# The first RMS norm of an encoder block, made on token rows in the load stage instead of on channel rows beside the first projection

## What is computed

```python
def rms_norm(x, gain):
    y = xf * lax.rsqrt(jnp.mean(xf * xf, axis=-1, keepdims=True) + NORM_EPS)
    return y * gain

def encoder_layer(h, ...):
    u = rms_norm(h, norm_mix)
    proj = u @ w_in
    dn_qkv, dn_z, dn_b, dn_a, at_q, at_k, at_v, gate_dn, gate_at = split_cols(proj, IN_SPLITS)
    ...
    merged = jax.nn.sigmoid(gate_dn) * y_dn + jax.nn.sigmoid(gate_at) * y_at
    h = h + merged @ w_o
```

## Time and profile before

| | us |
|---|---|
| median of 3 runs (3501.0 to 3505.09) | 3501.05 |
| the profiled execution | 3500.08 |
| its span, first to last instruction | 3498.3 |
| TensorE busy (84%) | 2953.3 |
| VectorE busy (46%) | 1623.2 |
| ScalarE busy (26%) | 899.2 |
| GpSimd busy (9%) | 313.1 |

### The profile page before, as it was taken

How to read it: one execution, slowest core, us unless ns; L and a number is a source line. 1 busy time by engine, 2 the same in 40 slices (tenths; PEclk the granted TensorE clock), 3 DMA queues, 4 the chain that set the end, 5 groups by cost and what they waited for, 6 DMA issues and landing times. The chain is left out here.

```text
span 3498.3 us, 41643 instructions
## 1 busy us (share of the span) xinstructions
PE 2953.3 (84%) x17373; PEld 2476.4 (71%) x17373; DVE 1623.2 (46%) x2172; ACT 899.2 (26%) x1233; POOL 313.1 (9%) x409
## 2 busy tenths in 40 slices
PE   5884216989476994899799989999999999999999
PEld 3663105878365773799788877888888888888877
DVE  5431322895934583243476733433333343434542
ACT  2553001111022451122244445123111111111331
POOL 0000110000000000666200022011000000000110
PEclk7887557999788996899999999999999999999999
DMA  2211455236132222766301046321111111111112
GB/s 89 69 45 43 114 140 163 82 126 180 43 80 68 75 93 79 195 181 183 113 31 46 16 158 235 126 80 36 37 37 37 37 37 42 38 37 37 46 52 58
DMA packets 298337, 295.58 MB, mean 84 GB/s; under 512 B 52635, under 2 KB 254006, under 8 KB 297270
## 3 DMA queue, kind: packets, MB, share of 16 engines
q1 hardware_dynamic: 291104, 257.66, 24.7%
q0 software_dynamic: 6096, 35.00, 2.9%
q10 hardware_dynamic: 966, 0.46, 0.1%
HBM read 205.67 MB, written 87.41 MB: 84 GB/s over the span
## 5 line engine op out<-in xcount | busy, mean ns | idle before, releaser
L366 PE MATMUL psum<-u_hi,w_hi 128*128 128x512 f32 x1296 | 337.6, 370 | 174.2 <-DVE w_lo L355 155.5
L1715 PE MATMUL psum<-x_hi,w_hi 128*128 128x512 f32 (+1 forms) x1536 | 385.8, 359 | 6.2 <-issue 4.7
L1715 PE MATMUL psum<-x_lo,w_hi 128*128 128x512 f32 (+1 forms) x1536 | 383.3, 358 | 0.0
L1715 PE MATMUL psum<-x_hi,w_lo 128*128 128x512 f32 (+1 forms) x1536 | 382.9, 357 | 0.0
L366 PEld LDWEIGHTS psum<-u_hi,w_hi 128*128 128x128 f32 x1296 | 221.8, 194 | 222.6 <-DVE w_lo L355 158.1
L1488 ACT ACTIVATE w_hi<-w_stage 128x1024 fp32r<-128x1024 f32 x96 | 101.6, 1058 | 926.3 <-PE psum L1715 913.4
L366 PE MATMUL psum<-u_lo,w_hi 128*128 128x512 f32 x1296 | 330.1, 364 | 0.0
L366 PE MATMUL psum<-u_hi,w_lo 128*128 128x512 f32 x1296 | 328.1, 362 | 0.0
L1998 DVE TENSOR_TENSOR tail_h<-tail_h,psum 128x1280 f32<-128x1280 f32 x136 | 202.0, 1485 | 248.8 <-PE psum L1715 248.6
L1715 PEld LDWEIGHTS psum<-x_hi,w_hi 128*128 128x128 f32 x1536 | 255.9, 188 | 52.1 <-issue 6.2
L1715 PEld LDWEIGHTS psum<-x_lo,w_hi 128*128 128x128 f32 x1536 | 255.3, 188 | 45.5
(11 more groups left out here) (231 smaller groups left out, 4295.2 us busy)
## 6 DMA issues: line engine op xcount, KB each, us to landing
w_stage<-in_w_in_dram SPq DMA_DIRECT2D x54, 512.0 KB, 4.1
w_stage<-in_w_up_dram SPq DMA_DIRECT2D x32, 512.0 KB, 4.0
w_stage<-in_w_down_dram SPq DMA_DIRECT2D x32, 512.0 KB, 3.8
dc_rows<-rows_gc_beta SPq DMA_DIRECT2D x40, 256.0 KB, 6.7
gates<-gate_buf SPq DMA_DIRECT2D x16, 640.0 KB, 5.5
st_v<-dn_v SPq DMA_DIRECT2D x20, 512.0 KB, 6.3
st_decay<-rows_decay SPq DMA_DIRECT2D x20, 512.0 KB, 7.5
dn_o<-st_ob SPq DMA_DIRECT2D x80, 128.0 KB, 2.0
```

Source lines behind the costliest of these rows:

```text
L366: ins = e.matmul(outs[c], w(k), x(k)[:, n0:n1], start=(k == 0 and n == 0), stop=(k == n_k - 1 and n == 2))
L1715: ins = e.matmul(acc_chunk(core, t % 2, c), wt[:, k, cols], x(k)[:, n0:n1], start=(k == 0 and n == 0), stop=(k == n_k - 1 and n == 2))
```

## The change

`phase_load` and `Norm` are replaced by one stage, `phase_head`, which runs ahead of the convolution stage and leaves `u_hi` and `u_lo` complete. It works token tile by token tile, with a token on each partition:

- SyncE issues all ten loads at once, each into a place of its own, the constants behind the first.
- ScalarE squares a row and accumulates its sum (`stat`), and takes the root of the mean of 128x1. VectorE takes the reciprocal of 128x1 and multiplies the rows by it and by the gain, which GpSimd's queue has broadcast to all partitions (`mix_gain`, 512 KB).
- TensorE turns the raw rows and the normed rows, eight 128x128 squares each, into PSUM, two slots for each kind. ScalarE takes the normed ones as the high part, VectorE subtracts for the low part.
- The raw ones are copied half by ScalarE, half by VectorE into `x_turned` (two slots), and SyncE stores each tile to `h_rows`; the pieces are 512 bytes long. The stage ends when all are stored.
- The parameter rows come on GpSimd's queue, are turned behind the fifth tile into a bank of the normed slots, and copied to `par`; the sixth tile's normed transposes wait for that.

`hT` and its store in the gate stage are gone, `h_rows` is written by the head. The class `Split`, which nothing used, is deleted. Line numbers behind the head are 15 to 20 lower.

```diff
-def phase_load(core, io, ct, hT):
...
+def phase_head(core, io, ct, u_hi, u_lo, d_hT):
     nc = core.nc
+    landed_const, landed_rows, landed_gain, params_ready, params_taken = (
+        core.sem(n) for n in ("const_landed", "rows_landed", "gain_landed", "params_ready", "params_taken"))
+    x_landed, h_stored = core.sems("x_landed", NT), core.sems("h_stored")
+    S = type("Sems", (), {n: core.sem(n) for n in ("squared", "rooted", "inverse", "normed", "raw_full", "norm_full", "raw_first", "raw_second", "hi_done", "lo_done", "eps_ready")})
     with ExitStack() as ctx:
         rows = sb(nc, ctx, "param_rows", [P, P])
+        xin = sb(nc, ctx, "x_in", [P, NT, D_MODEL])
+        gain = sb(nc, ctx, "mix_gain", [P, D_MODEL])
+        xn, junk = sb(nc, ctx, "x_normed", [P, 2, D_MODEL]), sb(nc, ctx, "x_squares", [P, D_MODEL])
+        stat = sb(nc, ctx, "x_stats", [P, NT, 2])
+        turned = sb(nc, ctx, "x_turned", [P, 2, KT, P])
+        raw = lambda t: core.psum[:, 1024 * (t % 2):1024 * (t % 2) + 1024]
+        normed = lambda t: core.psum[:, 2048 + 1024 * (t % 2):2048 + 1024 * (t % 2) + 1024]
+        split_k = lambda ap: ap.rearrange("p (k t) -> p k t", t=P)
+        own = lambda t: slice(t * P, (t + 1) * P)
+        HALF = KT // 2
         row_sources = [(PC_CONV, CONV * 16, io["dn_conv_w"].rearrange("a i (j p) -> (a i j) p", p=P)),
                        (PC_MIX, KT, io["norm_mix"].rearrange("a (j p) -> (a j) p", p=P)),
                        (PC_MLP, KT, io["norm_mlp"].rearrange("a (j p) -> (a j) p", p=P)),
                        (PC_QN + AH, AKV, io["k_norm"].rearrange("a p -> (a p)").partition_broadcast(AKV)),
                        (PC_QK, 2 * QKH, io["c_qk_scale"])]
         with nc.Block() as block:
+            @block.gpsimd
+            def _(e):
+                e.dma_start(gain[:, :], io["norm_mix"].rearrange("a d -> (a d)").partition_broadcast(P)).then_inc(landed_gain, 16)
                 for at, n, src in row_sources:
                     e.dma_start(rows[at:at + n, :], src).then_inc(landed_rows, 16)
             @block.sync
             def _(e):
+                for t in range(NT):
+                    src = io["x_prompt"][0, own(t), :] if t < NT_P else io["x_sample"][0, own(t - NT_P), :]
+                    e.dma_start(xin[:, t, :], src).then_inc(x_landed[t], 16)
+                    if t == 0:
+                        e.dma_start(ct["tri"][:, :, :], io["c_tri"].rearrange("n p c -> p n c")).then_inc(landed_const, 16)
+                for t in range(NT):
+                    e.wait_ge(S.raw_first, t + 1)
+                    e.wait_ge(S.raw_second, t + 1)
+                    e.dma_start(d_hT[:, :, own(t)], turned[:, t % 2, :, :]).then_inc(h_stored[t % 2], 16)
+                for s in range(2):
+                    e.wait_ge(h_stored[s], 16 * (NT // 2))
             @block.tensor
             def _(e):
+                def turn_raw(t):
+                    e.wait_ge(x_landed[t], 16)
+                    if t >= 2:
+                        e.wait_ge(S.raw_first, t - 1)
+                        e.wait_ge(S.raw_second, t - 1)
+                    for k in range(KT):
+                        ins = e.transpose(raw(t)[:, own(k)], xin[:, t, own(k)], ct["ident"])
+                    ins.then_inc(S.raw_full, 1)
+                def turn_normed(t):
+                    e.wait_ge(S.normed, t + 1)
+                    if t >= 2:
+                        e.wait_ge(S.lo_done, t - 1)
+                    if t == 5:
+                        e.wait_ge(params_taken, 1)
+                    for k in range(KT):
+                        ins = e.transpose(normed(t)[:, own(k)], xn[:, t % 2, own(k)], ct["ident"])
+                    ins.then_inc(S.norm_full, 1)
                 e.wait_ge(landed_const, 16)
+                for t in range(NT):
+                    turn_raw(t)
+                    turn_normed(t)
+                    if t == 4:
+                        e.wait_ge(landed_rows, 16 * len(row_sources))
+                        e.wait_ge(S.lo_done, 4)
+                        e.transpose(core.ps[7][:, 0:N_PC], rows[0:N_PC, :], ct["ident"][0:N_PC, 0:N_PC]).then_inc(params_ready, 1)
+            @block.scalar
+            def _(e):
+                def root(t):
+                    e.wait_ge(x_landed[t], 16)
+                    if t >= 1:
+                        e.wait_ge(S.squared, t)
+                    e.activation(junk[:, :], xin[:, t, :], ACT.Square, accum_out=stat[:, t, 0:1]).then_inc(S.squared, 1)
+                    e.wait_ge(S.squared, t + 1)
+                    e.activation(stat[:, t, 1:2], stat[:, t, 0:1], ACT.Sqrt, bias=ct["eps"][:, 0:1], scale=1.0 / D_MODEL).then_inc(S.rooted, 1)
+                def take(t):
+                    e.wait_ge(S.norm_full, t + 1)
+                    e.activation(u_hi[:, :, own(t)], split_k(normed(t)), ACT.Copy).then_inc(S.hi_done, 1)
+                    e.wait_ge(S.raw_full, t + 1)
+                    if t >= 2:
+                        e.wait_ge(h_stored[t % 2], 16 * (t // 2))
+                    e.activation(turned[:, t % 2, 0:HALF, :], split_k(raw(t))[:, 0:HALF, :], ACT.Copy).then_inc(S.raw_first, 1)
+                e.wait_ge(S.eps_ready, 1)
+                for t in range(NT):
+                    root(t)
+                    if t >= 1:
+                        take(t - 1)
+                take(NT - 1)
             @block.vector
             def _(e):
+                def norm(t):
+                    e.wait_ge(S.rooted, t + 1)
+                    e.reciprocal(stat[:, t, 1:2], stat[:, t, 1:2]).then_inc(S.inverse, 1)
+                    e.wait_ge(S.inverse, t + 1)
+                    if t >= 2:
+                        e.wait_ge(S.norm_full, t - 1)
+                    e.scalar_tensor_tensor(xn[:, t % 2, :], xin[:, t, :], stat[:, t, 1:2], gain[:, :], ALU.mult, ALU.mult).then_inc(S.normed, 1)
+                def take(t):
+                    e.wait_ge(S.raw_full, t + 1)
+                    if t >= 2:
+                        e.wait_ge(h_stored[t % 2], 16 * (t // 2))
+                    e.tensor_copy(turned[:, t % 2, HALF:, :], split_k(raw(t))[:, HALF:, :]).then_inc(S.raw_second, 1)
+                    e.wait_ge(S.hi_done, t + 1)
+                    e.tensor_tensor(u_lo[:, :, own(t)], split_k(normed(t)), u_hi[:, :, own(t)].bitcast(F32), ALU.subtract).then_inc(S.lo_done, 1)
+                e.memset(ct["eps"][:, :], EPS).then_inc(S.eps_ready, 1)
+                e.wait_ge(landed_gain, 16)
+                norm(0)
+                for t in range(1, NT):
+                    norm(t)
+                    take(t - 1)
+                    if t == 5:
+                        e.wait_ge(params_ready, 1)
+                        e.tensor_copy(ct["par"][:, 0:N_PC], core.ps[7][:, 0:N_PC]).then_inc(params_taken, 1)
+                take(NT - 1)
...
-class Norm(Source):
...
-class Split(Source):
...
-def phase_gates(core, io, wb, u_hi, u_lo, w_in, d_z, d_gate, d_at, d_u, hT, d_hT):
+def phase_gates(core, io, wb, u_hi, u_lo, w_in, d_z, d_gate, d_at, d_u):
...
-    out_stored, h_stored = core.sems("out_stored"), core.sem("h_stored")
+    out_stored = core.sems("out_stored")
...
                     e.wait_ge(acc, j + 3)
-                    if j == VH:
-                        e.dma_start(d_hT, hT[:, :, :]).then_inc(h_stored, 16)
                     dst = d_z[j] if j < VH else d_gate[j - VH]
                     e.dma_start(dst, buf[:, j % 2, :]).then_inc(out_stored[j % 2], 16)
                 for s in range(2):
                     e.wait_ge(out_stored[s], 16 * (N // 2))
-                e.wait_ge(h_stored, 16)
 
...
-        hT = sb(nc, ctx_m, "hT", [P, KT, TOK])
...
-        phase_load(core, io, ct, hT)
         with ExitStack() as ctx_a:
             u_hi = sb(nc, ctx_a, "u_hi", [P, KT, TOK], F32R)
             u_lo = sb(nc, ctx_a, "u_lo", [P, KT, TOK], F32R)
+            phase_head(core, io, ct, u_hi, u_lo, d_hT)
...
-                    norm = Norm(core, ct, hT, par[:, PC_MIX:PC_MIX + KT], u_hi, u_lo, sb(nc, c2, "n_tmp", [P, 2, TOK]), bufs[4][:, :])
-                    phase_gemm(core, wb, u_hi, u_lo, w_cols(w_in, C_Q), 2 * QKH, hooks_conv(ct, bufs, PC_CONV, d_qkT, tok_major(d_qk), True), source=norm)
+                    phase_gemm(core, wb, u_hi, u_lo, w_cols(w_in, C_Q), 2 * QKH, hooks_conv(ct, bufs, PC_CONV, d_qkT, tok_major(d_qk), True))
...
-                phase_gates(core, io, wb, u_hi, u_lo, w_in, d_z, d_gate, d_at, d_u, hT, d_hT)
+                phase_gates(core, io, wb, u_hi, u_lo, w_in, d_z, d_gate, d_at, d_u)
```

More of the change, by code:

```diff
@@ L209, in _ @@
-                e.wait_ge(landed_rows, 16 * len(row_sources))
-                e.wait_ge(bank_free, 2 * NT + 1)
-                e.transpose(core.ps[0][:, 0:N_PC], rows[0:N_PC, :], ct["ident"][0:N_PC, 0:N_PC]).then_inc(params_ready, 1)
+                def turn_raw(t):
[6 more added lines that the diff above has]
+                    ins.then_inc(S.raw_full, 1)
@@ L301 @@
-class Split(Source):
```

(20 more changed lines are left out.)

73 lines of the change are left out of this document (removed).

## The result

| | before | after |
|---|---|---|
| median of the runs, us | 3502.8 (4 runs, 3501.0 to 3505.09) | 3480.81 (4 runs, 3478.7 to 3483.6) |
| span of the profiled execution, us | 3498.3 | 3481.8 |
| first weight issue of the convolution stage | 33.38 | 48.18 |
| first product | 70.05 | 54.72 |
| third weight tile on ScalarE (reference point) | 91.71 | 71.12 |

The ratio is 0.9937, with a 95% interval of 0.992 to 0.9955: faster by 16 to 28 us. The direction was right, and so was the way it comes about: the norm leaves the path of the first products. The size was 22.0 us from median to median instead of 14.6. Of the 7.4 us between them, 1.7 come from a fourth run of the kernel before, which moved its median from 3501.05 to 3502.8; the other 5.7 are the changed kernel's own.

The account below looks back on a forecast made before the run. TensorE, busy 84%, bounds the whole; the first products wait on the norm. Removing 36.1 us, with the new head ending at 54.4, gains 14.7 us from 3500.08; plus 1 for the median, 3486.5 us, range 3482 to 3494.5.

Parts of the forecast that it names:

- The removed norm, 36.1 us of the path: Convolution stage: without norm and its splits, first weight issue to third weight tile takes 22.24 us instead of 58.33.
- The first token tile at 15.3 us: New head: rows there at 5 us, then norm, transposes, high and low part, done at about 15.3 us.
- The period, "I take 3.82": Head, each further token tile: 3.82 us, between VectorE's 3.6 and TensorE's 4.05 at 1.2 GHz.
- Nine full rounds: Head: the nine token tiles after the first each cost a full period, together 34.4 us.
- Handshake and buffers, 2.0 us: Head: sixth tile's wait for the parameters in the shared bank plus filling two-slot buffers, 2.0 us (1.5 to 3).
- The last store 2.7 us behind the last low part: End of the head: the last tile's store lands 2.7 us after the last low part.
- bounds for H, 52.3 and 56.2: Time the new head ends, forecast 54.4 us: 52.3 with TensorE at 2.4 GHz all the way, 56.2 at 1.2.
- Gain row at nothing: Head: broadcast on GpSimd's queue lands by 9 us, costing nothing; the late rival, up to 6 us, had chance 0.09.
- Parameter rows and the gate stage's store at zero: Parameter rows arrive before they are needed near 30 us; removing the gate stage's residual store gains nothing; both zero.
- TensorE at 1.2 GHz through the whole head: Rival, chance 0.20: head's transposes all at the low clock, head ends at 56.2 us, gain 12.9, time 3488.
- Stores setting the pace: Rival, chance 0.05: turned-tile slots wait for stores; at 11 us landing the period is 6.2 us, time 3508.
- Given back later: Rival, chance 0.06: later waits or clock moves return 8 us of the gain, leaving 3494.5 to 3501 us.

Follow-up runs that it names:

- the third trace: The changed kernel run again without an edit, a repeat; ScalarE takes up the third weight tile at 71.37 us.

## Why the prediction missed

- **The removed norm, 36.1 us of the path: right.** 58.33 - 22.94 = 35.4 us by the changed kernel's own stage; 33.3 for the norm proper and 2.1 for the splits by the run without the norm. The 0.7 us less is for the most part a longer start at 1.2 GHz: three products took 1.26 us or more until 59.15, 4.4 us behind the first, and only until 982.67, 3.3 us behind the first, in the value columns.
- **The first token tile at 15.3 us: 1.1 us too late.** Its rows were there at 4.2 us, not at 5, and the semaphores took less; the prediction's own terms sum to 15.1, so 0.2 of it stood in no term. The two table loads were 1.28 us each.
- **The period, "I take 3.82": this is the step that failed.** It was 3.12 us. The prediction priced VectorE's instructions well (3.3 us against 3.34), then added 0.3 us "with gaps and semaphores", where three of four neighbours in fact overlap; then it went up by another 0.2 towards TensorE's 4.05 us at 1.2 GHz. The runs with the raw tiles turned twice and with ScalarE taking both halves show that TensorE at 2.4 GHz has no part in the period and that the busiest engine's chain is all of it. Even where TensorE was at 1.2 GHz in the changed kernel, one round, from 25.84 to 28.95 us, stayed at 3.11. Over eight rounds the 0.70 us are 5.6 us.
- **Nine full rounds: one too many.** The last has no multiplication and took 1.72 us, 2.1 less than was counted.
- **Handshake and buffers, 2.0 us: too little.** The rounds above 3.12 us add 3.6 us: 0.7 in the first round, 1.5 for the first stores, 1.3 around the parameters.
- **The last store 2.7 us behind the last low part: right** (2.8). But from its landing to the first weight issue it took 0.9 us, not the 0.36 that the prediction kept from the old load stage.
- **The sum.** 5.6 + 2.1 - 1.6 = 6.1 us, and 1.1 for the first tile, less 0.6 for the end of the block: the 6.6 us by which the first weight issue came earlier than forecast. The prediction's bounds for H, 52.3 and 56.2, are 52.4 and 56.5 by its own terms, which changes nothing; the measured end lies far below both.
- **Gain row at nothing: right, but by luck as much as by reason.** It landed at 7.7 us and was needed at 8.3; in the third trace it came last and cost 0.4 us. By the run with the gain behind the parameters, each microsecond later would have cost nearly one.
- **Parameter rows and the gate stage's store at zero: right.**
- **TensorE at 1.2 GHz through the whole head: came for a part of it.** After transposes alone TensorE ran at 2.4 GHz in every trace of the changed kernel: eight took 1.04 to 1.09 us instead of 1.97. But every one of them also shows a stretch at 1.2 GHz, 21.5 to 28 us in the first and 24 to 33 us in the second, and the second's head ended 0.9 us later with it. The Trainium skill's rule (TensorE: Matmul & The Clock Gate, "Part 4: PE-mode transpose") that the high level doesn't engage for transposes is contradicted by these lengths. I expected TensorE at 2.4 GHz to fall back after rounds in which it works for 2.2 of 3.6 us; with 2.1 of 3.12 us, between 30 and 44 us, it did not.
- **Stores setting the pace: didn't come.** From the third on they landed after 3.5 to 3.8 us; the first took 7.1 us behind the loads and cost one wait.
- **Given back later: nothing that can be told** from a spread of 10 us in one and the same program.

## What to carry to other kernels

Before adding "gaps" to a sum of instructions of one engine, look at a place where the same engine runs such instructions back to back: if they overlap there, the sum is an upper bound. A pipeline of buffered stages then runs at the busiest engine's chain, not at a mean over the engines, as long as the other engines' parts fit into the slots; the run without the raw half shows a case where they did not. A transposition of layout pays when it moves a reduction and a slow operation from full width to one column: here the reciprocal went from 8.15 us to ten times 0.16. And after such a change look at the seam: loads, splits and stores at the stage's border were worth another 6.9 us, a third of what the change itself gave at the reference point, and two small waits inside the head 2.4 us more.

## What was not expected of the hardware

- Less work made TensorE slower: with eight transposes a round it stood at 1.2 GHz for 37 us in the one trace of that kernel. With sixteen it ran at 2.4 GHz from 15 to 20 us on, with one stretch of 3 to 10 us at 1.2 GHz in eight traces of ten; in the other two, and in the one with twenty-four, there was none.
- The granted clock's column shows 1.00 from the start of a trace until the first fall, also where the transposes' lengths are those of 1.2 GHz: in the fourth trace of the kernel before it does so through the whole load stage, where eight took 1.97 us throughout. A clock at the start of a trace is better read from lengths.
- Instructions of VectorE that don't wait for each other started 0.08 to 0.09 us before their forerunner's end (multiplication 36.63 to 37.91, copy from 37.83).
- The ten loads, the gain and the first stores together moved 385 to 394 GB/s between 6 and 20 us; the busiest stretch among the rows read before was 322 GB/s at a share of 0.80. It is not new in the changed kernel: the kernel before moved 402 GB/s between 4 and 6 us, with its first loads.
- Of one and the same program, four traces differ by 11 us in span (3494.3 to 3505.5 us).
